# Runs of unread products of ones on TensorE at ten borders of a transformer block

## The reference, cut to what matters

```python
h = rms_norm(x, norm1_g) * (1.0 + scale1) + shift1
p = h @ w_in
q, k, v, f_logit, p_rwkv, gate_logit = split(p)
o_fox = fox_attention(q, k, v, log_sigmoid(f_logit + b))
o_rwkv = rwkv7_branch(token_shift(p_rwkv, mu), ...)
merged = g_fox * (o_fox @ w_out_fox) + g_rwkv * (o_rwkv @ w_out_rwkv)
x = x + gate1 * (merged @ w_o)
h2 = rms_norm(x, norm2_g) * (1.0 + scale2) + shift2
y = hier_moe(h2, ...)            # 32 experts, top 2
out = rms_norm(x + gate2 * y, final_g)
```

## Time and profile before

| | |
|---|---|
| runs shown | 1892.78, 1894.09, 1897.73 us; median 1894.09 |
| the profiled execution | 1893.03 us; span 1891.3 us from first to last instruction |
| mean granted TensorE clock | 0.934 of full speed |
| busy: PE, PEld, DVE, ACT, POOL | 1700.5, 1397.5, 1218.4, 905.7, 429.1 us |
| stages by start in the trace | attend 541, recur 672, blend 963, outward 1076, route 1206, experts 1240 |
| HBM | 342.79 MB read, 70.33 MB written |

### The profile page before, as it was taken

The page is one execution under the profiler, slowest core; times in us unless marked ns, Lnnn a source line. Parts: engine busy times, 40 slices in busy tenths (PEclk is TensorE's granted clock), DMA queues, the critical chain, the costliest instruction groups (busy, mean ns, idle before and its releaser), DMA issues. The chain is left out here.

```text
span 1891.3 us, 31809 instructions
## 1 busy us (share of the span) xinstructions
PE 1700.5 (90%) x12190; PEld 1397.5 (74%) x12190; DVE 1218.4 (64%) x1567; ACT 905.7 (48%) x1315; POOL 429.1 (23%) x633
## 2 busy tenths in 40 slices
PE   5999999999989968988859899358999999999976
PEld 5788888887878846877848788247888888888862
DVE  4655355431047755777344555568999999999976
ACT  2631111222147734454321322047888888888861
POOL 0100111200020025656300011012233233233212
PEclk9999999999989978898679999669999999999998
DMA  9368666431447313131166123547899999999966
GB/s 330 123 211 292 219 211 227 158 110 46 111 116 161 103 53 66 44 75 28 25 214 217 51 100 112 224 183 290 339 386 392 383 385 387 376 381 386 381 260 262
DMA packets 150800, 397.96 MB, mean 210 GB/s; under 512 B 51298, under 2 KB 67713, under 8 KB 129185
## 3 DMA queue, kind: packets, MB, share of 16 engines
q1 hardware_dynamic: 119200, 328.77, 48.4%
q0 software_dynamic: 16736, 41.34, 6.1%
q10 hardware_dynamic: 14752, 26.29, 3.7%
HBM read 342.79 MB, written 70.33 MB: 218 GB/s over the span
## 5 line engine op out<-in xcount | busy, mean ns | idle before, releaser
L2683 DVE TENSOR_TENSOR ex_w_r<-w,ex_w_r 128x1024 fp32r<-128x1024 f32 x384 | 451.8, 1221 | 24.0 <-ACT ex_w_r L2614 11.2
L2614 ACT ACTIVATE ex_w_r<-w 128x1024 fp32r<-128x1024 f32 x384 | 404.1, 1063 | 110.2 <-PE psum L2543 87.3
L2541 PE MATMUL psum<-ex_w_r,ex_x_t 128*128 128x512 f32 x512 | 204.2, 399 | 4.0 <-DVE ex_x_t L2683 2.4
L2543 PE MATMUL psum<-ex_w_r,ex_x_t 128*128 128x512 f32 x512 | 201.0, 393 | 0.0
L2542 PE MATMUL psum<-ex_w_r,ex_x_t 128*128 128x512 f32 x512 | 200.7, 392 | 0.0
L555 ACT ACTIVATE stage<-psum 128x512 f32<-128x512 f32 (+1 forms) x72 | 41.4, 575 | 299.6 <-PE psum L157 181.8
L155 PE MATMUL psum<-w_even,h_hi 128*128 128x512 f32 (+1 forms) x320 | 118.7, 371 | 4.4 <-ACT stage L555 4.4
L2494 POOL COPY ex_idx<-row_pair 128x1 int32 (+1 forms) x32 | 34.3, 1073 | 372.7 <-ACT ex_y L2614 372.7
L156 PE MATMUL psum<-w_even,h_hi 128*128 128x512 f32 (+1 forms) x320 | 118.4, 370 | 0.0
L157 PE MATMUL psum<-w_even,h_lo 128*128 128x512 f32 (+1 forms) x320 | 118.3, 370 | 0.0
L2541 PEld LDWEIGHTS psum<-ex_w_r,ex_x_t 128*128 128x128 f32 x512 | 97.1, 190 | 23.9 <-DVE ex_x_t L2683 2.8
(11 more groups left out here) (430 smaller groups left out, 3928.5 us busy)
## 6 DMA issues: line engine op xcount, KB each, us to landing
w<-in_exp_w SPq DMA_DIRECT2D x128, 1024.0 KB, 13.6
w<-in_exp_w SPq DMA_DIRECT2D x32, 2048.0 KB, 8.6
w_ring<-in_ada_w SPq DMA_DIRECT2D x12, 2048.0 KB, 10.5
w_ring<-in_w_in SPq DMA_DIRECT2D x10, 2048.0 KB, 10.5
qk<-stage_r ACTq DMA_DIRECT2D x16, 512.0 KB, 7.8
gates<-stage ACTq DMA_DIRECT2D x32, 256.0 KB, 2.0
bl_gates<-gates SPq DMA_DIRECT2D x8, 1024.0 KB, 4.9
w<-pair_rows SPq DMA_DIRECT2D x16, 512.0 KB, 10.1
```

The lines of the kernel that those rows point to most:

```text
L2541: nc.tensor.matmul(out, lhs[0], hi, start=first, stop=False)
L2543: return nc.tensor.matmul(out, lhs[1], hi, start=False, stop=last)
L2614: return nc.scalar.activation(out, src, ACT.Copy)
L2683: return nc.vector.tensor_tensor(out, whole, high.bitcast(F32), ALU.subtract)
```

## The change

A helper keep_running issues n products of the ones by the first 512 columns of gate2 into a PSUM bank that holds nothing alive at that point. Nobody reads them, and they wait for nothing and signal nothing. It is called at ten places with 3, 16, 5, 4, 6, 10, 12, 4, 7 and 11 products, 78 in all.

```diff
--- before.py
+++ after.py
@@ -156,6 +156,13 @@
         nc.tensor.matmul(out, a_hi, b_lo, start=False, stop=False)
         last = nc.tensor.matmul(out, a_lo, b_hi, start=False, stop=(i == n - 1))
     return last
+
+
+def keep_running(nc, const, out, n):
+
+
+    for _ in range(n):
+        nc.tensor.matmul(out, const["ones"][:], const["gate_row"], start=True, stop=True)
 
 
 def front(nc, sig, bank, const, keep, ins, dram, weights):
@@ -846,6 +853,7 @@
                 at(n - 3, mix)
                 at(n - 2, flip(1, 1))
                 at(n, score(0))
+            keep_running(nc, const, bank[0], 3)
 
         @block.scalar
         def _(act):
@@ -1652,6 +1660,7 @@
                 at(t + 2, flip(3))
                 at(t, doubled(5, 0), doubled(5, 1))
                 at(t + 2, products(0))
+            keep_running(nc, const, bank[4], 16)
 
         @block.vector
         def _(dve):
@@ -1914,6 +1923,8 @@
             for s in range(TT + 1):
                 if s + 1 < TT:
                     flip(s + 1)
+                if s == 0:
+                    keep_running(nc, const, bank[2], 5)
                 if s < TT:
                     branches(s)
                 if s >= 1:
@@ -2088,10 +2099,12 @@
                     last = nc.tensor.matmul(bank[6][0:GE, 0:P], w_route[:, k, :], h_t[:, k, :], start=(k == 0), stop=(k == KT - 1))
                 last.then_inc(sig("logits_full"), 1)
 
+            keep_running(nc, const, bank[4], 4)
             for s in range(TT + 1):
                 if s < TT:
                     project_out(s)
                 if s == TT:
+                    keep_running(nc, const, bank[7], 6)
                     flip(s - 1)
                 if s >= 1:
                     router(s - 1)
@@ -2254,6 +2267,7 @@
 
         @block.tensor
         def _(pe):
+            keep_running(nc, const, bank[4], 10)
             pe.wait_ge(sig("rt_const"), 1)
             pe.wait_ge(sig("rt_both"), 1)
 
@@ -2261,6 +2275,7 @@
             nc.tensor.matmul(bank[0][:, 0:TT * E], before[:], all_tiles, start=True, stop=True).then_inc(sig("ranks"), 1)
             nc.tensor.matmul(bank[1][:, 0:TT * E], ones[:], all_tiles, start=True, stop=True).then_inc(sig("totals"), 1)
 
+            keep_running(nc, const, bank[4], 12)
             for j in range(2):
                 pe.wait_ge(sig("of_place"), 2 * (j + 1))
                 for t in range(TT):
@@ -2596,7 +2612,9 @@
                 if not behind:
                     down(blk, None, 0)
 
+            keep_running(nc, const, bank[6], 7)
             slots(pe, slot)
+            keep_running(nc, const, bank[4], 11)
             pe.wait_ge(sig("spread"), 2 * TT)
             for t in range(TT):
                 pe.wait_ge(sig(f"cb_rows_in{t}"), 32)
@@ -2779,6 +2797,7 @@
         const = {"ident": sb("ident", [P, P]), "ones": sb("ones", [P, P]), "neghalf": sb("neghalf", [P, H]), "psum": psum}
         keep = {"mod_bc": sb("mod_bc", [P, 5, D])}
 
+        const["gate_row"] = keep["mod_bc"][:, 3, 0:NC5]
         keep["c_silu"] = sb("c_silu", [P, KT])
         shared = {}
         for name, shape, dt in (("w_ring", [P, 2, KT, NC5], F32), ("qk_even", [P, 4, 2, S], F32R), ("tm_fm", [P, 2 * KT * NC5], F32),
```

## The result

The changed kernel took 1899.97 us in the median of 20 runs, the kernel before 1893.93 us in 20 runs beside them. The ratio is 1.0023 with a 95% interval of 1.0012 to 1.0034, so 4.4 us more (2.3 to 6.4). Measured twice more, at other times, the ratio was 1.0001 (0.9988 to 1.0013) and 1.0005 (0.9992 to 1.0018). All three intervals hold a difference of 2.3 us. The forecast was +0.8 us, within 0.3% of no change.

The account below looks back on a forecast made before the run. TensorE was taken as the bound in stages with dense matmuls, waiting at borders for VectorE, a gather or a store. Gains of about 7.5 and costs of about 8.3 gave +0.8 on 1894.09: 1894.9 us, range 1889 to 1901.5.

Parts of the forecast that it names:

- place 9: Experts' start, 7 products inside TensorE's wait: flip quicker, first up matmuls still low, -0.9 us; ends -0.9 and -3.0.
- slower: Outcome class for the whole kernel: a time over 1899.8 us, chance 0.20.
- Place 3: Blend, 5 products between flip(1) and branches(0): they stand ahead of ready work, +4.3 us; ends +4.3 and +6.
- Rival (b): Faster: flip(1)'s rows land before weights are split, 1888.9, or clock held further, 1889.4; chance of either 0.16.
- Places 2 and 8: Recur's end, 16 products, and route's end, 4 products: borders reached later, +1.0 and +3.0 us.
- Place 1: Attend's end, 3 products: border 0.4 us late, first logits 1.3 us quicker, net -0.9; ends +0.4 and -1.3.
- Place 4: Outward's start, 4 products: a run started low ends 1.7 us after the wait, net 0; ends -1.7 and +0.9.
- Place 5: Outward's last flip, 6 products in a 6.65 us wait: flip, router, last transposes quicker, -3.1 us; ends -3.1 and -0.9.
- Rival (a): Held clock is lost on the way to the work, so slower: +6.5 us, 1900.6; chance 0.17.
- a gap under 2.7 us is safe: Clock step for all runs: TensorE idling under 2.7 us keeps the clock, over 5.4 us does not.
- Places 6, 7 and 10: Route's start, after the totals, before the last sum (10, 12, 11 products, in waits): -0.9, 0 and -1.7 us.
- Rival (c): Products of ones do not lift or keep the clock: places late by together 52 us, 1946; chance 0.03.

Follow-up runs that it names:

- the two controls: The changed kernel measured again, unaltered, at two other times against the kernel before: ratios 1.0001 and 1.0005, 0.2 and 0.9 us slower.

## Why the prediction was right, and where it was not

The total came out as forecast, within 0.3% of no change, by the reasons given: losses at 2, 3 and 8 against gains at 5, 6, 9 and 10. The two halves were measured apart, -4.5 and +9.1 us. The size is less well met than it looks. The marks give +3.5 and not +0.8: places 1, 4 and 8 were 1.1, 1.3 and 0.7 us worse than forecast, place 9 was 0.9 better. The first measurement, +4.4, was nearer to the mark I had set for "slower" (+5.7) than to the forecast, and the two controls, +0.2 and +0.9, lay close to it. That the misses did not add up to more is in part luck.

- **Place 3** was the largest term and is the best shown: +4.3 forecast, +4.4 in the trace, its wait found unfilled, and removed by the move ahead of flip(1), which gains 0.5 to 1.6 us once the late flip is taken off. Rival (b)'s first condition, rows that land before the weights are split, fails on the 6.36 us row.
- **Places 2 and 8**: +1.0 and +3.0 forecast, +1.2 and +3.7 measured, within both ends. Place 8 was sized with a clock that rises 3.4 us after the start; here it rose after 4.4, and the border came 3.7 late.
- **Place 1**: -0.9 forecast, -0.6 mostly. The border was 0.6 late for the 0.4 reckoned, and the clock had fallen again by the logits in the first trace (1.07 each).
- **Place 4** (forecast 0) fails on one step: "it ends 1.7 us after the wait does". That holds only when the clock rises early. In the execution shown the run was low from first to last, four products in 6.07 us, the stage began 2.5 late and won back 1.2. In another the same four took 4.6 us, and the sum was -0.2. The +1.3 lies outside the ends I gave (-1.7 and +0.9). The 1.7 I added to every run that starts low was one execution's; how long such a run takes differs from execution to execution, and in a wait that barely holds it at full speed it is a bet.
- **Place 5**: -3.1 forecast, -2.9 when it works. Rival (a), the clock lost on the way to the router, was the truth in four of the seven executions with six products. This is such a one, the changed kernel's third measurement:

```profile
1194.37 5.42 PE L165 MATMUL psum<-mod_bc,ones 128*128 128x512 f32 x12
1201.15 1.09 PE L2088 MATMUL psum<-ident,ow_h_mid 128*128 128x128 f32 x8 [1.36 <-DVE ow_h_mid L2169]
1203.36 3.33 PE L2099 MATMUL psum<-ow_h_t,w_route 128*36 128x128 f32 x16 [1.11 <-ACT ow_h_t L2119]
```

  The idle times are those of the first execution to 0.01 us (1.36 and 1.11), and the router takes 3.33 for 1.94. So "a gap under 2.7 us is safe" was wrong as a step. The trace of the kernel before had a counterexample that I did not read:

```profile
1072.79 1.09 PE L1910 MATMUL psum<-ident,bl_mixed 128*128 128x128 f32 x8 [1.24 <-DVE bl_mixed L1982]
...
1074.00:1076.00 2.00, 0.00 (x0) 0.00 (x0) 0.00 (x0) 1.31 (x2) 0.00 (x0) 0.94 0.00 0
```

  TensorE stopped at 1073.9, and 0.94 puts the fall at 1075.8, 1.9 us later; ahead of its last eight transposes it had idled for 1.24. (The upper end was misread too: rows 5 give 5.2 us from 1189.96 to 1195.2, not 5.4.) Nor do the rows say what decides in place of the gap: the two executions of place 5 have the same run, the same flip and the same idle times. One product in the 1.11 us gap made the router 1.94 in three of three; three of the seven without it had 1.94 as well, so this alone is thin evidence. Rival (a) left the place -0.9; with the clock lost it gave -1.3 to -1.6. As a rival for the whole kernel (a) was half true, and I gave it too little for single places and treated it as one event for all of them.
- **Transposes.** By the Trainium skill (TensorE: Matmul & The Clock Gate, Part 4: PE-mode transpose) transposes do not count as work for the clock gate. The two traces disagree, for float32 transposes of 128x128 back to back: 73 of them kept the clock for 8.1 us, and 60 raised it. So their kind alone does not explain why the clock was lost at places 4, 5 and 9. That the idle times around the few transposes there did it was not tested: they were not varied by themselves.
- **Places 6, 7 and 10**: -0.9, 0 and -1.7 forecast, and measured so in every execution that had the products.
- **Place 9**: -0.9 forecast; -1.8 in the first trace, +0.9 in the worst. My assumption that the first up products start low was right (0.79). That the flip is quick was not always: it took 1.95 to 1.97 us in three executions, behind a run at full speed and 2.1 to 2.4 us of idling, and 1.04 to 1.10 in five others with the same seven products, three of them behind 2.2 to 2.4 us of idling as well. The rest of the spread stands in the first two blocks of experts and was not traced further.
- **Rival (c)**, products of ones that do not lift the clock, is out: once the clock is up they step by 0.86 us at nine of the ten places. At place 4, in the execution shown, it rose only as the run ended.

## What to carry to other kernels

An unread product costs nothing only where TensorE has nothing ready behind it: look at the idle time in front of the very instruction that follows the call, not at the stage's. Between a flip that waited and branches that were ready, five products cost 4.4 us; one instruction earlier they gained 0.5 to 1.6, although they ended up to 1.4 us after the rows had landed. At the end of a stage they hold up the border of all engines, so their count must end before the last other engine's arrival. And it seems surer to put one or two products in every short gap on the way to the work than a long run some gaps earlier: with them the router and the first up products ran at full speed in three executions of three, without them the router in three of seven and the up products in none. Three executions are few, and what exactly keeps the clock is not shown.

## What I had not expected

- Runs that begin at the low clock needed from 3.0 us (place 3) to 6.0 us (place 4) to raise it, with the same products.
- Idle times of the same length (2.47 and 2.54 us, 1.36 and 1.35 us) ended with a low clock in one execution and a full one in another.
- Transposes served as well as products at places 5 and 10, in one execution: 0.11 us each, so they also fill a gap more finely than the 0.86 us of a product.
- Moving every run into a wait beats both kernels, by 12 us against the kernel before, and by 15 to 16.5 with five products more at attend's start.
